# Modulation rows of a fused transformer kernel: weighted by VectorE beside the projections instead of by TensorE between attention units

## What is computed

```python
mod = jax.nn.silu(c) @ w_ada[l] + b_ada[l]
sh1, sc1, g1, sh2, sc2, g2 = jnp.split(mod, N_MOD, axis=-1)
h = rms_norm_2(x, norm1_g[l]) * (1.0 + sc1[:, None]) + sh1[:, None]
...
x = x + g1[:, None] * mix
h = rms_norm_2(x, norm2_g[l]) * (1.0 + sc2[:, None]) + sh2[:, None]
```

## Time and profile before

| | |
|---|---|
| median of 3 runs | 978.06 us (977.4 to 981.19) |
| the profiled execution | 980.98 us |
| its span, first to last instruction | 978.9 us |
| PE busy | 817.0 us, 83% of the span |
| DVE busy | 308.2 us, 31% |
| ACT busy | 170.8 us, 17% |
| mean granted PE clock | 0.935 of full |
| read from memory | 282.75 MB |

### The profile page before, as it was taken

How to read it: one execution, slowest core, us unless ns; L and a number is a source line. 1 busy time by engine, 2 the same in 40 slices (tenths; PEclk the granted TensorE clock), 3 DMA queues, 4 the chain that set the end, 5 groups by cost and what they waited for, 6 DMA issues and landing times.

```text
span 978.9 us, 13367 instructions
## 1 busy us (share of the span) xinstructions
PE 817.0 (83%) x5617; PEld 477.2 (49%) x5617; DVE 308.2 (31%) x786; ACT 170.8 (17%) x477; POOL 39.7 (4%) x36
## 2 busy tenths in 40 slices
PE   5999899999999899998887998686777767587665
PEld 3544554455567544455454755353444535354332
DVE  1476541127755423125443121211211111111112
ACT  3121540213255401004111010000000000000001
POOL 0110000011600000000000000000000000000000
PEclk9999998999999999999997999897998889998789
DMA  9963791243502475445465999999999999999994
GB/s 345 393 241 121 276 344 59 96 166 118 200 35 98 150 253 187 172 171 204 147 234 213 428 384 428 428 429 428 428 428 428 429 428 428 428 428 427 428 426 163
DMA packets 53387, 284.39 MB, mean 291 GB/s; under 512 B 2656, under 2 KB 7136, under 8 KB 40416
## 3 DMA queue, kind: packets, MB, share of 16 engines
q1 hardware_dynamic: 53344, 283.81, 73.2%
HBM read 282.75 MB, written 1.05 MB: 290 GB/s over the span
## 4 chain that ended last, share of the span: by engine, by line
PE 56%; DMA 33%; DVE 4%; ACT 2%; issue 2%; POOL 1%; SPq 1%; DVEq 0%; POOLq 0%
DMA ring<-in_up_w 30%; PE banks L1627 14%; PE banks L1748 14%; PE banks L2049 7%; PE banks L1707 4%; DMA ring<-in_down_w 3%; PE banks L1729 2%; PE banks L1654 2%; PE banks L1691 2%; PE banks L2095 2%; PE banks L1735 1%; POOL rs L512 1%; DMA ring<-in_ab_w 1%; PE banks L1606 1%; PE banks L2032 1%
## 5 line engine op out<-in xcount | busy, mean ns | idle before, releaser
L2049 PE MATMUL banks<-ring,QT 128*32 128x256 f32 x1952 | 148.1, 451 | 85.4 <-DMA ring<-in_up_w 84.6
L1748 PE MATMUL banks<-ring,hT 128*128 128x512 f32 (+4 forms) x384 | 157.3, 564 | 5.0 <-DMA ring<-in_ab_w 2.5
L2049 PEld LDWEIGHTS banks<-ring,QT 128*32 128x32 f32 x1952 | 78.1, 125 | 153.0 <-issue 95.1
L1627 PE MATMUL banks<-ring,hT 128*128 128x512 f32 x320 | 141.1, 600 | 7.5 <-ACT hT L536 5.1
L1748 PEld LDWEIGHTS banks<-ring,hT 128*128 128x128 f32 x384 | 72.2, 192 | 76.8 <-issue 68.8
L1627 PEld LDWEIGHTS banks<-ring,hT 128*128 128x128 f32 x320 | 60.9, 192 | 82.8 <-issue 76.7
L1518 DVE TENSOR_TENSOR QT<-banks,MOD 32x256 f32<-32x256 f32 x128 | 53.8, 420 | 140.3 <-PE banks L2095 139.0
L2095 PE MATMUL banks<-ring,QT 128*32 128x256 f32 x992 | 68.3, 420 | 15.6 <-ACT QT L828 12.4
L1509 DVE TENSOR_TENSOR QT<-QT,banks 64x256 f32<-64x256 f32 x32 | 13.5, 423 | 198.0 <-ACT QT L821 198.0
L512 POOL TENSOR_TENSOR rs<-st,mhalf 128x1 f32<-128x1 f32 (+7 forms) x27 | 32.5, 1204 | 933.7 <-DVE st L1561 467.1
L821 ACT ACTIVATE QT<-banks 64x256 f32<-64x256 f32 x32 | 12.0, 375 | 299.9 <-PE banks L2049 299.9
(11 more groups left out here) (344 smaller groups left out, 693.5 us busy)
## 6 DMA issues: line engine op xcount, KB each, us to landing
ring<-in_up_w SPq DMA_DIRECT2D x31, 2048.0 KB, 23.4
ring<-in_gate_w SPq DMA_DIRECT2D x30, 2048.0 KB, 18.9
ring<-in_down_w SPq DMA_DIRECT2D x30, 2048.0 KB, 21.8
ring<-in_ada_w SPq DMA_DIRECT2D x12, 2048.0 KB, 9.0
ring<-in_ab_w SPq DMA_DIRECT2D x4, 2048.0 KB, 20.2
ring<-in_cd_w SPq DMA_DIRECT2D x4, 2048.0 KB, 9.4
ring<-in_in_w SPq DMA_DIRECT2D x4, 2048.0 KB, 11.2
ring<-in_ab_out_w SPq DMA_DIRECT2D x2, 2048.0 KB, 10.5
```

What stands on the lines that cost most here:

```text
L1627: ins = pe.matmul(bank[j % 4][:, 0:n], hT[:, k, t * P:(t + 1) * P], w[:, k, :], start=(k == 0), stop=(k == KD - 1))
L1748: ins = pe.matmul(bank[b][:, 0:n], hT[:, k, t * P:(t + 1) * P], w[:, k, :], start=(k == 0), stop=(k == KD - 1))
L2049: return pe.matmul(bank[1][CAP * j:CAP * j + CAP, 0:256], XG[:, k, CAP * s:CAP * s + CAP], wk[:, :, 2 * (j % 2):2 * (j % 2) + 2], start=(k ...
```

## The change

PE no longer multiplies by silu(c). DVE does it: for chunk c, `weigh(c)` multiplies each of the 8 slices of the weights (128x512) by a column of silu(c) and adds it to an accumulator in `extra`, 8 instructions. PE then adds the 128 partitions with one product by a matrix of ones (`ada_sum`), and DVE adds the result into MOD as before. These stand beside the projections: `weigh(0)` before attention part 0, 1 to 4 around `about`, 5 and 6 at the start of the CD projections, 7 to 9 around `cdout`, 10 and 11 around `win`. Attention units have no modulation work but one `ada_sum(0)` in unit 3. The list of loads is reordered accordingly, and a chunk's slot is now freed by `weigh`, whose last instruction raises `ada_mm`.

```diff
-        add_ada(0, 7)
+        add_ada(0, 1)
         add_cols("about", ab_out_w, D)
+        add_ada(1, 7)
         for c in range(3):
             add_piece("cdin", cd_w, CD_AT, CD_WIDTHS, c)
...
         chunks.append(("scratch", [], ("dq_T", 8)))
-        add_ada(7, 10)
         add_cols("cdout", cd_out_w, D)
+        add_ada(7, 8)
         chunks.append(("rows", [(0, D, 1, norm_rows[:, 0:1]), (D, D, 1, norm_rows[:, 2:3])], ("final_row", 1)))
-        add_cols("win", in_w, 2048)
-        add_ada(10, 11)
+        add_ada(8, 10)
+        add_cols("win", in_w, 2048, (0, 2))
+        add_ada(10, 12)
+        add_cols("win", in_w, 2048, (2, 4))
...
+            def weigh(c, ks=range(KD)):
+
+                if ks[0] == 0:
+                    arrived(v, f"ada{c}")
+                    if c > 1:
+                        v.wait_ge(*upto("ada_s", c - 1))
+                w = weights(f"ada{c}")[:, :].rearrange("p (k n) -> p k n", k=KD)
+                acc = ada_acc(c)
+                for k in ks:
+                    by = cs[:, 1, k:k + 1]
+                    if k == 0:
+                        ins = v.tensor_scalar(acc, w[:, k, :], by, None, ALU.mult)
+                    else:
+                        ins = v.scalar_tensor_tensor(out=acc, in0=w[:, k, :], scalar=by, in1=acc, op0=ALU.mult, op1=ALU.add)
+                    link(ins, "ada_mm" if k == KD - 1 else "dve")
...
-            add_and_norm("about", "cd", "cdx", col="cd_col")
+            def beside_first(n):
+                if n == 0:
+                    weigh(2)
+                elif n == 1:
+                    ada(1)
+                    weigh(3)
+                elif n == 2:
+                    ada(2)
+                elif n == 3:
+                    weigh(4, range(0, 4))
+                elif n == 4:
+                    ada(3)
+                elif n == 6:
+                    weigh(4, range(4, 8))
...
-            attention(0, ada_during)
+            attention(0, fill=lambda u: ada_sum(0) if u == 3 else None)
...
-            project("about", D, first_outputs)
+            project("about", D, first_outputs, ada_sums({1: 1, 2: 2, 3: 3}))
...
             for t in range(NT):
                 cd_rows(t)
                 project_cd(0, t, t)
+            pe.wait_ge(*upto("about_x", 4))
+            ada_sum(4)
             project_cd(1, 0, 0)
+            ada_sum(5)
             pe.wait_ge(*upto("cdin_Pv", 1))
             turn_into(4, tr(CD["kc0"]) + tr(CD["kc1"]), "cda_T")
             project_cd(1, 1, 1)
+            ada_sum(6)
...
-            project("cdout", D, second_outputs)
+            project("cdout", D, second_outputs, ada_sums({1: 7, 2: 8, 3: 9}))
...
-            project("win", 2048, normed_rows("e1", "e1x"))
+            project("win", 2048, normed_rows("e1", "e1x", 9), ada_sums({1: 10, 3: 11}))
```

More of the change, by code:

```diff
@@ L583, in evac_PT, with attention @@
                 act.activation(PTB[:, u % 2, 0:nb, :], banks[:, 4:4 + nb, :], ACT.Copy).then_inc(sem("ptA"), 1)
-            def attention(part, ada=lambda u: None, after=lambda u: None, early=lambda: None):
+            def attention(part, after=lambda u: None, early=lambda: None):
                 lo, hi = U0[part], U0[part + 1]
@@ L1043, in ada, with expert_rows @@
                 cols = mod_flat[:, 512 * c:512 * c + 512]
[L1044 to L1054, removed]
+                link(v.tensor_tensor(cols, cols, ada_bank(c)[:, :], ALU.add), "ada_v")
+            def expert_rows(u):
+                if u == U0[3]:
+                    arrived(v, "pool")
+                    link(v.scalar_tensor_tensor(out=MOD[:, 4, :], in0=MOD[:, 4, :], scalar=1.0,
+                                                in1=weights("pool")[:, 2560:2560 + D], op0=ALU.add, op1=ALU.mult),
+                         "G_rows")
             def latent_sums(t):
@@ L1202, in _ @@
             choose_keys(1)
+            weigh(0)
             evacuated(5, 0)
             evacuated(5, 1)
-            attention(0, after=ada_rows)
-            for t in range(NT):
-                turned_rows("abm", t)
-            add_and_norm("about", "cd", "cdx", col="cd_col")
+            attention(0, after=lambda u: ada(0) if u == 4 else None)
+            turned_rows("abm", 0)
+            weigh(1)
+            turned_rows("abm", 1)
+            def beside_first(n):
[12 more added lines that the diff above has]
+                    weigh(4, range(4, 8))
+            add_and_norm("about", "cd", "cdx", col="cd_col", beside=beside_first)
+            weigh(5)
+            ada(4)
+            weigh(6)
+            ada(5)
             pe = small("pe")
@@ L1366, in _ @@
                 go(v.tensor_copy(QT[0:96, 2 * j:2 * j + 2, :], bank[4 + j % 4][0:96, :]), "dq_Tv")
-            attention(2, after=ada_rows)
-            for t in range(NT):
-                turned_rows("cdm", t)
+            attention(2)
+            turned_rows("cdm", 0)
+            weigh(7)
+            turned_rows("cdm", 1)
             a = SM["lambdas"][0]
@@ L1629, in project, with normed_rows @@
                         ins.then_inc(sem(tag + "_mm"), 1)
[L1631 removed]
+                        beside(j)
+            def normed_rows(name, tag, chunk=None):
                 def ready(t):
                     pe.wait_ge(*upto(name + "_xn", t + 1))
+                    if t == 1 and chunk is not None:
+                        pe.wait_ge(*upto("ada_v", chunk + 1))
                     turn_rows(tag, 0, t)
@@ L1709, in finish_unit, with attention @@
                 ins.then_inc(sem("pv"), 1)
-                if c is not None:
-                    ada_sum(c)
-            def attention(part, ada=lambda u: None, fill=lambda u: None, early=lambda: None):
+            def attention(part, fill=lambda u: None, early=lambda: None):
                 lo, hi = U0[part], U0[part + 1]
```

97 lines of the change are left out of this document (53 added, 44 removed).

## The result

The changed kernel takes **996.12 us** (median of 4 runs, 992.68 to 999.14), the kernel before 979.40 beside it (4 runs, 977.4 to 981.19): a ratio of 1.017, 95% interval 1.0128 to 1.0212, so slower by 1.3 to 2.1%. Forecast were 984.7 and a range of 973 to 995. The profiled execution is the slowest of the four; its span is 997.1 us, 18.2 more than before.

A forecast was written before the change was run, and what follows sets the result against it. PE's chain in the front was taken to set the end, before a fixed-length expert stretch. Terms: -21.8 + 9.1 + 13.1 + 2.0 + 2.5 + 1.8 = +6.7 us, median 978.06 to about 984.7; range 973 to 995.

The forecast's parts named there:

- The ring: Likeliest case: the ring of loads takes again some 22 us that attention gives; 979 to 991 us, chance 0.55.
- the stretch of experts: Late in the kernel, transfers of a fixed number of bytes: the same length, only moved by the front.
- Wait for `cdin0`: Before the first cdin tile: cdin0 queues behind ada6 and PE waits, costing 13.1 us (12.4 to 15.2).
- Ten sums: Between projection tiles: ten of PE's twelve sums over the partitions, at 0.91 us, add 9.1 us on the path.
- The weighing: DVE's weighing, 6.2 us a chunk, fits beside PE's tiles or in idle time; nothing charged.
- Wait for ada10: Second passage, cdout to win: PE waits for chunk 10's weighing before its sum, 2.5 us (0 to 5).
- Attention's gain: Parts 0, 2 and 3 without modulation gain 12.4, 5.5 and 3.9 us, together 21.8; bounds 32 and 17.
- model of a unit: Attention: a round over DVE, ACT and PE covers two units in 7.3 to 8.6 us; 4.2 a unit taken.
- the cold tile: First cdin tile: begins at the lower clock after PE idles 11 us, costing 2.0 us.
- one more fall: Attention, 16 units nearly unfilled: one added fall of PE's clock, 1.8 us (0 to 5).
- three signs of being wrong: Wrong if the cdin0 gap is under 8 us, part 0 over 38 us, or weighing over 1 us an instruction.
- third rival: Clock swings in unfilled attention parts: 1000 us at 1.2 GHz throughout, 992 with half the time low; chance 0.15.

The follow-up runs named there:

- Experiment 11: Kernel of experiment 7 with every sum over the partitions, and VectorE's addition, cut from 512 to 32 columns: 952.08 us.
- experiment 5: Changed kernel with six of the eight products of each weighing left out and the eighth cut to 32 columns: 989.41 us.
- experiment 7: Changed kernel with cdin0, cdin1, ada7 and ada10 loaded earlier, plus unread sums of constants on PE in seven attention units: 961.05 us.
- experiment 9: Changed kernel, its own order of loads, plus unread sums of constants on PE in seven attention units: 985.62 us.
- experiment 4: Kernel before, its order of loads kept, modulation left out of the attention units but for one product of 32 columns a chunk: 962.99 us.
- Experiment 3: Kernel before, with SP also waiting for the fourth about tile before issuing cdin0; modulation stays on PE in attention: 985.89 us.

## Why the prediction was wrong in size, by its own steps

- **Direction and place were right.** The ring takes back what attention gives, at `cdin0` and at ada10, and the stretch of experts is only moved (-2.4).
- **Wait for `cdin0`, 13.1 us**: measured 13.5. `cdin0` landed 15.1 us after ada6's issue, where 14.8 was taken.
- **Ten sums, 9.1 us**: 0.86 each, 8.6 together for the ten on PE's path (all but chunk 0's, in part 0, and chunk 3's, in the gap). Experiment 11 bears the term out.
- **The weighing, nothing charged**: right (experiment 5).
- **Wait for ada10, 2.5 us (0 to 5)**: 4.7, inside its bounds. The chunk landed 17.2 us after the last `cdout` tile's end where 14.8 was taken; PE was ready after 18.5, as forecast.
- **Attention's gain, 21.8 us**: 15.8, outside its lower bound of 17. This is the step that failed, and not by its model of a unit. That model, 34.2, 16.8 and 15 us for the parts, is met or beaten where the clock stays at 1.00: 33.15, 16.31 and 13.77 in experiment 7, 33.16 and 16.30 in experiment 9, 16.52 in part 2 of experiment 4. What it left out is that with the waits of 1 to 2 us, which it counted as idle time only, the granted clock falls to 0.50 for the `pv` groups, transposes and turned rows after them: `pv` 3.67 us for 2.00. With the waits filled (experiments 7 and 9) it does not, in parts 0 and 2.
- **Clock, 2.0 for the cold tile and 1.8 for one more fall**: the rows show 3.0 at the first `cdin` tile, 2.0 at the first `cdout` tile, 0.8 for the turned rows ahead of it (2.60 us from the part's end to the tile, for 1.83), and 2.9 behind the stall, 8.7 in all for 3.8. The 2.0 came from the kernel's first tile of 452 columns, which was a poor stand-in.
- **None of the three signs of being wrong came in**: the gap was 15.2 us, part 0 took 37.96 for a limit of 38, an instruction of the weighing 0.752 us. Only the one on part 0 could have caught the lower clock in attention, and it missed by 0.04 us.

Of the 11.5 us between the sum of +6.7 and the measured +18.2, attention's gain is 6.0, the clock behind the parts and stalls 4.9, the wait for ada10 2.2; the small terms take back some 2.

The prediction took one more fall of the clock for sixteen units, since the row at 462 to 464 spoke against the one at 148. Experiment 3 shows how little such a row says: that same fall came in one execution and not in another. Measured against experiment 9, the clock in and behind the bare units is worth 10.5 us, and without it the changed kernel takes 985.6, next to the 984.7 forecast. That it comes so close is partly luck: the three parts take 64.2 us there for 66.0 in the forecast, the cold tile 10.15 and the two tiles behind the stall 14.94 for 13.73. The case that came in is the third rival, 992 to 1000 us, given a chance of 0.15. Its mechanism holds in part: the clock was not low throughout (0.82 to 0.89 over the parts), but fell in a spell at the end of each part, and behind parts 0 and 2 stayed down into the next stage; and the spell slowed the `pv` groups too, which the rival had not counted. The Trainium skill, page "TensorE: Matmul & The Clock Gate", section "A second HAM failure mode: psum-queue depth-cycling", says that short idles between groups of matmuls swing the clock between two levels and that the cost is paid between bursts; the trace agrees on the swing, with 0.50 from some 133.6 to 147.3 beside idle stretches of 1 to 2 us, but here most of the cost is paid inside the groups (`pv` 3.67 for 2.00).

Not settled: why one unit's idle stretch brings the fall and the same stretch in another execution does not (part 2 without filler took 18.95 us at 0.82 in the changed kernel and 16.30 at 1.00 in experiment 5), and why small filler gives nearly all of the gain in four executions of six. The +1.0 ahead of part 0 and the -2.4 of the rest were not followed up.

## What to carry to other kernels

Work that is moved off a busy engine may have been what kept its clock up: price the units without it at both clock levels, and look at the rows of the tile behind them. Then fill the waits that are laid bare with products that nobody reads; here seven small fillers gave 10.5 and 12.5 us. And when a change reorders a queue that waits for slots, write down for each load which slot it waits for and what stands ahead: four loads that were moved ahead by one or two places were worth 22 us.

## What was not expected of the hardware

- The cold price. Sixteen matmul instructions of 128x512 take 6.87 to 7.11 us at the upper level and 10.07 to 10.15 behind an idle stretch of some 13.5 us, beginning at 0.50; one `pv` group of sixteen takes 2.00, and 3.67 at 0.50.
- The fall outlasts its cause. After an idle stretch of 1.8 us PE worked at 0.50 for some 13.7 us, mostly busy.
- Two loads of 2 MB issued within 0.6 us of each other landed 9.6 and 14.5 us after their issues; one with nothing ahead of it took 8.0, and ada10 behind `win1` 16.5.
